# Last two experts' outputs kept on chip in one stacked product, and the read-back of the others moved ahead, in a hybrid encoder block with a top-2 MoE

## The reference

```python
# t: 512 tokens x 1024, 32 experts of width 256, two of them for each token
for e in range(N_EXPERTS):
    hid = jax.nn.silu(t @ w_exp_gate[e]) * (t @ w_exp_up[e])
    out = out + combine[:, e:e + 1] * (hid @ w_exp_down[e])
x = x + out
return rmsnorm(x, norm_final_g)
```

## Time and profile before

| what | us |
|---|---|
| three timed executions | 806.68, 803.66, 807.12 |
| their median | 806.68 |
| the profiled execution, its own time | 803.49 |
| its span in the profile | 801.7 |
| PE busy | 749.6 (94% of the span) |
| DVE, ACT, POOL busy | 341.3, 256.0, 300.7 |
| moved by DMA | 166.60 MB, mean 208 GB/s |

### The profile page before, as it was taken

How to read it: one execution, slowest core, us unless ns; L and a number is a source line. 1 busy time by engine, 2 the same in 40 slices (tenths; PEclk the granted TensorE clock), 3 DMA queues, 4 the chain that set the end, 5 groups by cost and what they waited for, 6 DMA issues and landing times.

```text
span 801.7 us, 14079 instructions
## 1 busy us (share of the span) xinstructions
PE 749.6 (94%) x5523; PEld 600.6 (75%) x5523; DVE 341.3 (43%) x805; ACT 256.0 (32%) x462; POOL 300.7 (38%) x346
## 2 busy tenths in 40 slices
PE   5999999999999999999999999979999999988885
PEld 5887788878878877888888887856677767766651
DVE  6466643285684861435425333661221222111126
ACT  5343233361532767322304255521111111110012
POOL 3774525441520453244453244443333333232111
PEclk9999999999999999999999999999999999999998
DMA  9856742411220522383486295589999999999976
GB/s 256 158 110 123 215 129 54 105 36 20 53 54 6 139 66 54 87 228 83 80 181 183 53 304 227 204 284 384 389 387 389 400 387 387 381 393 383 389 300 249
DMA packets 74346, 166.60 MB, mean 208 GB/s; under 512 B 18838, under 2 KB 46310, under 8 KB 66344
## 3 DMA queue, kind: packets, MB, share of 16 engines
q1 hardware_dynamic: 65856, 150.34, 59.1%
q0 software_dynamic: 5392, 9.61, 3.5%
q10 hardware_dynamic: 3032, 5.74, 2.3%
HBM read 156.98 MB, written 16.97 MB: 217 GB/s over the span
## 4 chain that ended last, share of the span: by engine, by line
PE 73%; DMA 10%; DVE 10%; issue 2%; POOL 2%; ACT 2%; SPq 1%; ACTq 0%; DVEq 0%; POOLq 0%
PE bank L1076 13%; PE bank L1078 12%; PE bank L1077 12%; PE bank L1069 12%; PE bank L1425 10%; DMA arena<-in_w_exp_up 9%; PE bank L1435 5%; PE bank L1412 3%; DMA arena<-y_half 1%; PE bank L1447 1%; PE bank L1117 1%; DVE rows L1864 1%; DVE rows L1865 1%; DVE rt L2187 1%; PE bank L1227 1%
## 5 line engine op out<-in xcount | busy, mean ns | idle before, releaser
L877 POOL TENSOR_TENSOR ring_low<-ring,w_high 128x512 fp32r<-128x512 f32 (+1 forms) x64 | 81.4, 1272 | 117.1 <-ACT w_high L1517 113.1
L1076 PE MATMUL bank<-h_hi,w_high 128*128 128x512 f32 x296 | 119.5, 404 | 0.0
L1425 PEld LDWEIGHTS bank<-arena,hT 128*64 128x64 f32 x1728 | 98.4, 138 | 23.5 <-issue 12.5
L1077 PE MATMUL bank<-h_lo,w_high 128*128 128x512 f32 x296 | 115.7, 391 | 0.0
L1425 PE MATMUL bank<-arena,hT 128*64 128x128 f32 x1728 | 102.3, 276 | 7.9 <-DMA arena<-in_w_exp_up 6.0
L877 POOL TENSOR_TENSOR w_low<-ring,w_high 128x512 fp32r<-128x512 f32 x56 | 75.9, 1355 | 59.1 <-ACT w_high L1517 55.0
L2183 DVE SCALAR_TENSOR_TENSOR rt<-rt,bank 128x128 f32<-128x128 f32 x32 | 9.2, 287 | 174.1 <-ACT rt L1750 174.1
L1517 ACT ACTIVATE w_high<-ring 128x2048 fp32r<-128x2048 f32 (+1 forms) x32 | 58.8, 1836 | 58.2 <-PE bank L1078 39.3
L1078 PE MATMUL bank<-h_hi,ring_low 128*128 128x512 f32 x168 | 66.5, 396 | 0.0
L1076 PEld LDWEIGHTS bank<-h_hi,w_high 128*128 128x128 f32 x296 | 55.7, 188 | 14.4 <-issue 3.5
L1077 PEld LDWEIGHTS bank<-h_lo,w_high 128*128 128x128 f32 x296 | 55.7, 188 | 11.0
(11 more groups left out here) (334 smaller groups left out, 1358.8 us busy)
## 6 DMA issues: line engine op xcount, KB each, us to landing
arena<-in_w_exp_gate SPq DMA_DIRECT2D x27, 1024.0 KB, 13.5
arena<-in_w_exp_up SPq DMA_DIRECT2D x27, 1024.0 KB, 17.0
arena<-in_w_exp_down SPq DMA_DIRECT2D x27, 1024.0 KB, 19.2
ring<-in_w_in SPq DMA_DIRECT2D x33, 512.0 KB, 6.6
ring<-in_w_exp_gate SPq DMA_DIRECT2D x5, 1024.0 KB, 14.0
ring<-in_w_exp_up SPq DMA_DIRECT2D x5, 1024.0 KB, 17.3
ring<-in_w_exp_down SPq DMA_DIRECT2D x5, 1024.0 KB, 20.2
xres<-in_x SPq DMA_DIRECT2D x8, 512.0 KB, 7.1
```

The lines of the kernel that those rows point to most:

```text
L877: after(pool.tensor_tensor(low, full, high, ALU.subtract), w_lo if kk == KD - 2 else step["pool"])
L1076: pe.matmul(o, l_hi, r_hi, start=(n == 0), stop=False)
L1077: pe.matmul(o, l_hi, r_lo, start=False, stop=False)
L1425: ins = pe.matmul(bank[CAP * half:CAP * half + CAP, 1, P * n:P * n + P], xgT[:, x, kk, :], w[:, kk, P * half:P * half + P], start=(kk == 0 ...
```

## The change

1. `FIRST_OWN = 30`: the last two experts (31st and 32nd) are not scattered. Their down product (`own_down_rows`) writes both halves of the columns on the same 64 partitions, into banks 4 and 5: partitions 0 to 63 for the 31st, 64 to 127 for the 32nd. ACT copies the two banks after the 32nd.
2. The own products take 128 slots, those of both experts, on all rows of the array.
3. `y_total` counts 30 experts, so the read-back waits for the scatter of the 30th.
4. DVE makes the slot matrix for two experts (eight instructions in place of five), and `y_weight` inside the loop.
5. PE's order after the loop: rows of tile 2, own products of tiles 0, 2 and 1, rows of tile 3, own product of tile 3. DVE adds the own product to tiles 0 and 1 after the rows.

```diff
-LAST_EXPERT = EXPERTS - 1
+FIRST_OWN = EXPERTS - 2
@@ def y_total(b)
-            return 16 * len(range(b, LAST_EXPERT, DEEP))
+            return 16 * len(range(b, FIRST_OWN, DEEP))
@@ gpsimd
-            for e in range(EXPERTS - LAG, LAST_EXPERT):
+            for e in range(EXPERTS - LAG, FIRST_OWN):
                 put(e // UNROLL, e % UNROLL)
@@ tensor
+            def own_down_rows(b):
+                down, slots = expert_parts(b)[2], slice(CAP * b, CAP * b + CAP)
+                for half in range(2):
+                    for kk in range(2):
+                        ins = pe.matmul(bank[slots, 4 + half, :], hidT[:, CAP * kk:CAP * kk + CAP],
+                                        down[:, kk, 512 * half:512 * half + 512], start=(kk == 0), stop=(kk == 1))
+                ins.then_inc(down_done, 1)
@@ expert(i, b, turn_next, turn_last)
-                pe.wait_ge(y_sb, e1)
+                pe.wait_ge(y_sb, min(e1, FIRST_OWN) + (2 if e1 > FIRST_OWN else 0))
                 pe.wait_ge(down_loaded[b], 16 * i + 16)
-                down_rows(b, 4 + b % 2, down_done)
+                if e1 > FIRST_OWN:
+                    own_down_rows(b)
+                else:
+                    down_rows(b, 4 + b % 2, down_done)
@@
-                    pe.wait_ge(own_made, 5)
+                    pe.wait_ge(own_made, 8)
@@ after the loop
-            pe.wait_ge(own_token_ready, 1)
-            pe.wait_ge(y_sb, EXPERTS + 2)
-            for t in range(NT):
-                for half in range(2):
-                    s = slice(CAP * half, CAP * half + CAP)
-                    ins = pe.matmul(sum_banks(t)[:, half, :], own_token[s, t, :], ysb[s, LAST_EXPERT % DEEP, :], start=(t < 2), stop=(t < 2), skip_group_check=True)
-                if t < 2:
-                    ins.then_inc(own_summed, 1)
-            pe.wait_ge(weights_ready, 1)
-            for t in (2, 3):
+            def add_y(t):
                 for j in range(2):
                     pe.wait_ge(y_in[t][j], 16)
                     for half in range(2):
-                        ins = pe.matmul(... stop=(j == 1), ...)
-                ins.then_inc(summed, 1)
+                        ins = pe.matmul(... stop=False, ...)
+            def add_own(t, half):
+                return pe.matmul(sum_banks(t)[:, half, :], own_token[:, t, :], ysb[:, half, :], start=(t < 2), stop=True, skip_group_check=True)
+            pe.wait_ge(weights_ready, 4)
+            add_y(2)
+            pe.wait_ge(own_token_ready, 1)
+            pe.wait_ge(y_sb, EXPERTS + 1)
+            add_own(0, 0)
+            add_own(2, 0)
+            pe.wait_ge(y_sb, EXPERTS + 2)
+            add_own(0, 1).then_inc(own_summed, 1)
+            add_own(2, 1).then_inc(summed, 1)
+            add_own(1, 0)
+            add_own(1, 1).then_inc(own_summed, 1)
+            add_y(3)
+            add_own(3, 0)
+            add_own(3, 1).then_inc(summed, 1)
@@ scalar, act_experts
+                    if e1 == FIRST_OWN + 1:
+                        act.wait_ge(own_turned, 1)
+                        nc.scalar.activation(own_token, bank[:, 0, :]..., ACT.Copy).then_inc(own_token_ready, 1)
+                        continue
                     act.wait_ge(down_done, e1)
+                    if e1 == EXPERTS:
+                        for half in range(2):
+                            act.wait_ge(y_out[half], y_total(half))
+                            nc.scalar.activation(ysb[:, half, :], bank[:, 4 + half, :], ACT.Copy).then_inc(y_sb, 1)
+                        continue
@@ vector, own_slots: eight instructions
+                for j in range(2):
+                    tt(own_gain[j], oh[j][:, :, FIRST_OWN:EXPERTS], of_token, ALU.mult)
+                for n in range(2):
+                    tt(own_slot[:, :, n], at_slot[0], gains(0, n), ALU.mult)
+                for n in range(2):
+                    tt(at_slot[n], at_slot[1], gains(1, n), ALU.mult)
+                for n in range(2):
+                    tt(own_slot[:, :, n], own_slot[:, :, n], at_slot[n], ALU.add)
@@ vector, dve_experts
+                    if e1 == EXPERTS:
+                        y_weights()
@@ vector, after the loop
             def add(t):
                 for j in range(2):
                     dve.wait_ge(y_in[t][j], 16)
-                    ins = stt(... , res_ready if j else step["dve"])
+                    after(stt(...))
+                dve.wait_ge(own_summed, t + 1)
+                after(tt(halves, halves, sum_banks(t), ALU.add), res_ready)
-            for t in range(2):
-                add_own(t)
```

More of the change, by code:

```diff
@@ L487, in program @@
         y_weight = spare_row.rearrange("p (j t l) -> p j t l", j=2, t=2)
-        own_gain = [cut(NT), cut(NT)]
+        own_gain = [cut(2 * NT, "p (t n) -> p t n", t=NT) for _ in range(2)]
         junk_e = cut(EXPERTS)
@@ L1047, in _ @@
                     pool.sem_inc(gathering, 1)
-                    scatter(y_idx[0], 0, more_out)
+                    scatter(y_idx[0], DEEP - 1, more_out)
                     pool.wait_ge(more_out, n * 16 + 16)
@@ L1507, in _ @@
                     for half in range(2):
-                        ins = pe.matmul(sum_banks(t)[:, half, :], y_weight[:, j, t - 2, :], y_rows(t, j)[:, 512 * half:512 * half + 512], start=False, stop=(j == 1), skip_group_check=True)
-                ins.then_inc(summed, 1)
+                        ins = pe.matmul(sum_banks(t)[:, half, :], y_weight[:, j, t - 2, :], y_rows(t, j)[:, 512 * half:512 * half + 512], start=False, stop=False, skip_group_check=True)
+            def add_own(t, half):
[14 more added lines that the diff above has]
+            add_own(3, 1).then_inc(summed, 1)
         @block.scalar
@@ L1750, in act_experts @@
                     nc.scalar.activation(gate_th, bank[:, 1, 0:P], ACT.Tanh, scale=0.5).then_inc(gth_ready, 1)
+                    if e1 == FIRST_OWN + 1:
+                        act.wait_ge(own_turned, 1)
+                        nc.scalar.activation(own_token, bank[:, 0, :].rearrange("p (t l) -> p t l", t=NT), ACT.Copy).then_inc(own_token_ready, 1)
+                        continue
                     act.wait_ge(down_done, e1)
-                    if not isinstance(i, int) or i * UNROLL + b >= DEEP:
+                    if e1 == EXPERTS:
[3 more added lines that the diff above has]
+                        continue
+                    if e1 > DEEP:
                         act.wait_ge(y_out[y], i * (16 * UNROLL // DEEP) + 16 * (b // DEEP))
                     nc.scalar.activation(ysb[:, y, :], bank[:, 4 + b % 2, :], ACT.Copy).then_inc(y_sb, 1)
-                    if isinstance(i, int) and i * UNROLL + b == LAST_EXPERT - 1:
-                        act.wait_ge(own_turned, 1)
-                        nc.scalar.activation(own_token, bank[:, 0, :].rearrange("p (t l) -> p t l", t=NT), ACT.Copy).then_inc(own_token_ready, 1)
             for b in range(2):
@@ L1775, in _ @@
                     act.wait_ge(more_pe, n * 4 + 5)
-                    nc.scalar.activation(ysb[:, 0, :], bank[:, 4, :], ACT.Copy).then_inc(more_y, 1)
+                    nc.scalar.activation(ysb[:, DEEP - 1, :], bank[:, 4, :], ACT.Copy).then_inc(more_y, 1)
             for b in range(DEEP):
@@ L2162, in own_slots, with y_weights @@
             def own_slots():
-                gains = lambda j: own_gain[j].rearrange("p (t o) -> p t o", o=1).to_broadcast([P, NT, CAP])
-                twice = lambda one: one.rearrange("p t (o s) -> p t o s", o=1).to_broadcast([P, NT, 2, CAP])
+                gains = lambda j, n: own_gain[j][:, :, n:n + 1].to_broadcast([P, NT, CAP])
                 for j in range(2):
[L2167 to L2170, removed]
-                dve.wait_ge(own_made, 4)
-                tt(own_slot, twice(at_slot[0]), twice(at_slot[1]), ALU.add).then_inc(own_made, 1)
+                    of_token = wgt[j].rearrange("p (t o) -> p t o", o=1).to_broadcast([P, NT, 2])
+                    tt(own_gain[j], oh[j][:, :, FIRST_OWN:EXPERTS], of_token, ALU.mult).then_inc(own_made, 1)
+                dve.wait_ge(own_made, 2)
+                for n in range(2):
+                    tt(own_slot[:, :, n], at_slot[0], gains(0, n), ALU.mult).then_inc(own_made, 1)
+                dve.wait_ge(own_made, 4)
+                for n in range(2):
+                    tt(at_slot[n], at_slot[1], gains(1, n), ALU.mult).then_inc(own_made, 1)
+                for n in range(2):
+                    dve.wait_ge(own_made, 5 + n)
+                    tt(own_slot[:, :, n], own_slot[:, :, n], at_slot[n], ALU.add).then_inc(own_made, 1)
+            def y_weights():
+                dve.wait_ge(own_turned, 1)
+                for j, t in itertools.product(range(2), (2, 3)):
+                    ts(y_weight[:, j, t - 2, :], ident, wgt[j][:, t:t + 1], None, ALU.mult).then_inc(weights_ready, 1)
             def dve_experts(i, count):
@@ L2179, in dve_experts @@
                         turned_by_gains(b % 2).then_inc(turned_sb, 1)
```

(10 more changed lines are left out.)

## The result

Slower, and by almost what was forecast: a median of 811.01 us over five executions (809.74 to 811.68) against 806.44 for the kernel before (803.66 to 807.12). The ratio is 1.006, with a 95% interval of 1.0042 to 1.0078; on 806.4 us that is 3.4 to 6.3 us more, 4.8 in the middle. Forecast were 5.3 us more, 810.5 us.

A forecast was written before the change was run, and what follows sets the result against it. DMA reads set the end with PE under 1 us behind, so PE's time decides: 1.76 + 1.76 - 0.7 + 2.5 = +5.3 us on a mean of 805.2 gives 810.5 us, range 806 to 813.5.

The forecast's parts named there:

- The bound: Kernel's end before: DMA reads set it, PE less than 1 us behind, waiting 0.5 us ahead of (3,0) and (3,1).
- Down products: 31st's and 32nd's down products on PE: each 3.70 us in place of 1.94, +1.76 us twice.
- the argument on halves: Down products: earlier pairs use different array halves, full-width products sharing one never pair; so 3.70 us, not 1.94.
- Nothing covers the 31st's: After the 31st's down product: slot transposes and 32nd's gate product queue behind on PE, so all +1.76 us is paid.
- Rival C: 32nd's weights land later than 772.7, so the 31st's extra time falls in an existing wait: +3.5 us, 808.7; 9%.
- The gap: PE's wait for ACT's copy after the loop: 0.79 us before, taken as 0.1 with tile 2's rows first; -0.7 us.
- From there to the last sum: After the gap, to tile 3's sum: 16 full-width matmuls, 14.02 us in place of 11.50; +2.5 us.
- The reads: Read-back of `y_half`: issued from 772.8, 4.1 us earlier, landing before PE wants it; buys only what is already counted.
- rival D: Tile 2's rows after the loop: reads (2,0) or (2,1) late, holding PE's tail; two us more, +7.3, 812.5; 8%.
- The cover: DVE's slot matrix and ACT's copies hidden, costed at nothing; tile 1's sums on DVE end 1.3 us clear of the end.
- rival A: Last reads land later than profiled, lengthening the kernel before: change faster (5%), or 5.3 us partly made good, about 808 (10%).
- Rival B: One-sided down products of the 31st and 32nd overlap after all: +1.8 us in place of +5.3, 807.0; 8%.

The follow-up runs named there:

- e4: Kernel before with only the last two down products made one-sided: 31st's gate product to tile 3's sum 30.33 us against 27.65, ratio 1.0021.
- e5: Kernel before with only the eight own products made full height: 31st's gate product to tile 3's sum 30.13 us against 27.65, ratio 1.002.
- e1: Changed kernel with the last two down products paired across column halves again: median 806.33 us, ratio 1.0007 to the kernel before.
- e8: Changed kernel with the 31st's down product put off and done jointly with the 32nd's, matmuls in turn: median 810.58 us, ratio 1.0067 to the kernel before.
- e11: Kernel before, unedited, profiled once more: 31st's gate product to tile 3's sum 28.21 us against 27.65, median 806.36 us.
- e6: Changed kernel with PE's order undone, own products of tiles 0 and 1 first: median 811.41 us, ratio 1.007 to the kernel before.
- e2: Changed kernel with the read-back issued some 2.5 us later, after the row weights: median 809.92 us, ratio 1.0055 to the kernel before.
- e3: Changed kernel with the read-back issued 5.5 us later, after the 32nd's tanh: median 811.42 us, ratio 1.0073 to the kernel before.
- e9: e8 plus two idle full-width matmuls on PE during the wait for the 32nd's weights: median 808.31 us, ratio 1.0029 to the kernel before.
- e10: e9 plus tile 2's rows added by DVE in place of PE: median 806.14 us, ratio 1.0006 to the kernel before.

## Why the prediction was right

*The bound.* "DMA sets the end, but PE is less than 1 us behind" held: e4 and e5 each turned it with one edit. One reading was loose: PE itself was held up once, by 0.72 us, not twice by 0.5. The weight loads for (3,0) came 0.28 us late (0.52 in place of 0.24), but the six matmuls ran through in 5.42 us, which is 6 x 0.86 + 0.26. The sum doesn't use the two waits: its +2.5 comes from 11.50 and 14.02, and holds 0.72 for the wait and 0.20 for the passage from half-height products to full-height ones (784.57 - 780.93 = 3.64 where eight in pairs make 3.44; 3.63 in e4).

*Down products.* Predicted 3.70 us each, +1.76 twice; measured 3.65, +1.71 twice. The bounds were 1.94 and 3.70, and the choice by the argument on halves was right (e1). The Trainium skill's rule that different tiles multiply in parallel (TensorEngine Tiling (Array Packing), Key Properties) agrees with the trace: two tiles' products run together, even those of different experts (e8). That one tile's follow each other is what the runs add.

*Nothing covers the 31st's.* Right: the 32nd's gate product started 1.72 us later relative to the 31st's (775.61 - 765.95 = 9.66 against 7.94). Rival C is out. In e8 to e11 the weights let that product start 8.1 us after the 31st's, so in some executions up to 0.2 us may be covered.

*The gap.* Taken at 0.1 us, measured none; e6 puts its worth at 0.8. With it the part from the 32nd's down product to the rows came out 0.2 us shorter than predicted: 0.85 more than before in place of 1.06.

*From there to the last sum.* Predicted 14.02 us, measured 14.00 (784.67 to 798.67).

*The reads.* Predicted from 772.8, measured 774.20, which is 773.0 on the clock of before. No wait on PE, so rival D is out, and e2 shows the slack. That "the earlier read-back buys only what is already counted" is shown for 2.5 of the 3.8 us; "unmoved it would be there just in time too" is near, by the estimate from e3 some 0.4 us too good.

*The cover.* DVE's eight instructions and ACT's copies cost nothing, as costed; DVE's last own sum of tile 1 ended at 796.2, and ACT's square of it at 797.42, 1.25 us ahead of PE's last sum (1.3 predicted).

*The sum.* +5.3 predicted, +5.07 against the profile of before, about +4.5 against its three profiles. The term that was mis-sized is the waits on reads in the kernel before: 0.7 us in the profile, some 0.5 more in the mean. That is rival A, right in its mechanism and too small to turn anything. Rival B is out (e1).

*The time.* That 810.5 lies only 0.5 us from the median is partly luck. The base of 805.2 was 1.2 us under the 806.44 that the kernel before came to, and the 5.3 was 0.7 above the 4.6 measured; the two errors have opposite signs. The stretch carries the argument, not the sum with the base.

## What to carry to other kernels

Before a layout is changed to save a transfer, look at which half of the array each small product uses: two products of 64 columns, or of 64 rows, cost one while they alternate between halves, and full price each on the same half. Here giving that up twice cost 6.8 us of PE's time, for waits (on ACT's copy and on the reads) that were worth 1.8 us in the profile of before and some 2.3 in the mean of three. Whether two products on one half followed by two on the other still overlap was not tried. Where one engine is a microsecond behind the bound, cost the change on that engine, instruction by instruction, rather than on the resource that it relieves.

Compare stretches inside the profile by an anchor just ahead of the change, and take more than one profile of the kernel before.

## What the runs showed that I had not expected

- Removing 3.65 us of PE work from in front of a weight wait made the next product 2.4 us longer, by the clock; two matmuls without use won it back (e8, e9).
- POOL's small operations on 128x2 values took 1.3 us more when DVE ran a 128x1024 operation on two inputs in SBUF at the same time (e10), and nothing more beside one with an input in PSUM.
- The stretch repeated within 0.01 us where PE sets the end (32.72 and, with later reads, 32.71), and spread over 1.1 us where the read-back does (27.65, 28.21, 28.78).
